# The first loads of a two-layer decoder step: smaller pieces, in another order

## The reference, cut to what matters

```
def rmsnorm(x, g):
    y = xf * rsqrt(mean(xf * xf, axis=-1) + RMS_EPS)
    return y * g

hn = rmsnorm(x, ln_mix[l])
z = hn @ w_in[l]                 # q, k, v, recurrent x, gate y, two merge gates
...                              # window attention, gated linear recurrence, merge
x = x + merged @ w_out[l]
x = x + swiglu(rmsnorm(x, ln_ffn))      # layer 0; top-2-of-8 experts in layer 1
```

## Time and profile before

| | us |
|---|---|
| median of 3 runs | 1344.1 (1343.88 to 1344.44) |
| the profiled execution, its device time | 1344.15 |
| its span from the first to the last instruction | 1342.2 |
| PE busy (matmul) | 1331.5, 99% |
| PEld busy (weight load) | 1238.8, 92% |
| DVE busy | 1053.0, 78% |
| ACT busy | 811.2, 60% |
| POOL busy | 114.2, 9% |

### The profile page before, as it was taken

One profiled execution on the slowest core, in us unless ns is written; L12 is line 12 of the kernel. 1 busy time (PEld: TensorE's weight loads), 2 busy tenths in 40 slices (PEclk: granted clock), 3 DMA queues, 4 the chain that ended last, 5 costly groups with the idle time before them and its releaser, 6 DMA issues.

```text
span 1342.2 us, 23980 instructions
## 1 busy us (share of the span) xinstructions
PE 1331.5 (99%) x8393; PEld 1238.8 (92%) x8393; DVE 1053.0 (78%) x1660; ACT 811.2 (60%) x1218; POOL 114.2 (9%) x118
## 2 busy tenths in 40 slices
PE   9999999999999999999999999999999999999997
PEld 8999999999999999999999999998888888888886
DVE  6869878876666664456698889759999999999987
ACT  6466577435333333343566784358888888888885
POOL 3200000002000000000100000021012012022010
PEclk9999999999999999999999999999999999999999
DMA  7543354445444444444533544587999999999993
GB/s 254 178 127 100 110 174 141 147 143 178 144 147 145 141 141 142 141 141 142 161 111 95 177 153 147 170 345 249 406 400 396 399 387 372 391 394 367 400 359 140
DMA packets 83258, 297.21 MB, mean 221 GB/s; under 512 B 9568, under 2 KB 11104, under 8 KB 83168
## 3 DMA queue, kind: packets, MB, share of 16 engines
q1 hardware_dynamic: 77904, 278.19, 58.3%
q0 software_dynamic: 5120, 17.67, 4.4%
q10 hardware_dynamic: 144, 0.14, 0.0%
HBM read 284.45 MB, written 11.51 MB: 221 GB/s over the span
## 4 chain that ended last, share of the span: by engine, by line
PE 97%; DVE 1%; DMA 1%; ACT 0%; issue 0%; SPq 0%; DVEq 0%; ACTq 0%
PE ps L1535 20%; PE ps L1537 20%; PE ps L1536 20%; PE ps L1876 10%; PE ps L1880 10%; PE ps L1877 10%; PE ps L1698 1%; PE ps L1635 1%; PE ps L1912 1%; PE ps L1611 1%; PE ps L1651 1%; PE ps L1867 0%; PE ps L1758 0%; DMA x<-x_in 0%; PE ps L1606 0%; PE ps L1649 0%
## 5 line engine op out<-in xcount | busy, mean ns | idle before, releaser
L1059 DVE TENSOR_TENSOR mwlo<-mraw,mwhi 128x1024 fp32r<-128x1024 f32 x290 | 343.8, 1222 | 30.4 <-ACT mwhi L577 25.7
L977 DVE TENSOR_TENSOR wlo<-raw,whi 128x1024 fp32r<-128x1024 f32 x204 | 250.3, 1228 | 125.6 <-ACT whi L577 118.6
L577 ACT ACTIVATE mwhi<-mraw 128x1024 fp32r<-128x1024 f32 x290 | 303.8, 1060 | 57.1 <-PE ps L1880 55.3
L577 ACT ACTIVATE whi<-raw 128x1024 fp32r<-128x1024 f32 (+1 forms) x208 | 216.9, 1045 | 194.8 <-DMA raw<-w_mix 128.9
L1535 PE MATMUL ps<-xuh,whi 128*128 128x336 f32 x576 | 183.7, 319 | 1.1 <-DVE xul L990 1.1
L1536 PE MATMUL ps<-xul,whi 128*128 128x336 f32 x576 | 181.7, 315 | 0.0
L1537 PE MATMUL ps<-xuh,wlo 128*128 128x336 f32 x576 | 181.5, 315 | 0.0
L1535 PE MATMUL ps<-xnh,whi 128*128 128x336 f32 (+1 forms) x544 | 174.6, 321 | 0.0
L1537 PE MATMUL ps<-xnh,wlo 128*128 128x336 f32 (+1 forms) x544 | 171.0, 314 | 0.0
L1536 PE MATMUL ps<-xnl,whi 128*128 128x336 f32 (+1 forms) x544 | 170.8, 314 | 0.0
L1876 PE MATMUL ps<-mwhi,xeh 128*128 128x512 f32 x384 | 152.9, 398 | 0.2 <-ACT xeh L577 0.2
(11 more groups left out here) (333 smaller groups left out, 2570.3 us busy)
## 6 DMA issues: line engine op xcount, KB each, us to landing
mraw<-w_moe SPq DMA_DIRECT2D x292, 512.0 KB, 8.3
raw<-w_mix SPq DMA_DIRECT2D x159, 512.0 KB, 3.5
raw<-w_ffn SPq DMA_DIRECT2D x72, 512.0 KB, 3.5
tok_d<-xt POOLq DMA_DIRECT2D x6, 224.0 KB, 3.3
ysum_d<-zero POOLq DMA_DIRECT2D x3, 448.0 KB, 11.2
ysum<-ysum_d POOLq DMA_DIRECT2D x3, 448.0 KB, 10.5
o_y<-nt SPq DMA_DIRECT2D x8, 160.0 KB, 1.9
kc<-kc_in POOLq DMA_DIRECT2D x2, 512.0 KB, 6.3
```

What stands on the lines that cost most here:

```text
L577: return nc.scalar.activation(out, in_, ACT.Copy)
L977: v.tensor_tensor(wlo[slot(c)][:, :, :], raw[slot(c)][:, :].rearrange("p (k n) -> p k n", n=P), f32(whi[slot(c)][:, :, :]), ALU.subtract). ...
L1059: v.tensor_tensor(mwlo[q % MRING][:, :, :], mraw[q % MRING][:, :].rearrange("p (k n) -> p k n", n=512), f32(mwhi[q % MSPLIT][:, :, :]), AL ...
```

## The change: what it does

The first loads are cut smaller and put in another order.

- The first half of `raw0` becomes two quarters with two tiles of `x` behind each, and the second half comes then. Tiles 2 and 3 of `x` come one by one, tiles 4 and 5 and tiles 6 and 7 in pairs as before. `raw1` comes in two halves. SP issues 11 DMAs up to the end of `raw1` instead of 8, with the same bytes.
- ACT, DVE and PE take chunk 0 in three pieces (tiles 0 and 1, 2 and 3, 4 to 7) instead of two; the first half of chunk 1 waits for its own load.
- ACT loads only 8 parameter columns first. The rest of `par` is loaded by POOL in two DMAs ahead of `kc`, `vc` and `stin`. POOL now waits for `raw1` too before its first DMA. ACT waits for the rest of `par` ahead of the root, DVE ahead of the first use.
- PE runs 8 products with zeros instead of 11.

```
-N_WARM = (11, 11, 3)
+N_WARM = (8, 11, 3)
+X_PARTS = (1, 1, 1, 1, 2, 2)
+X_PART = (0, 1, 2, 3, 4, 4, 5, 5)
...
-            sy.dma_start(raw[0][:, 0:512], w_mix[0, 0, :, 0:512]).then_inc(raw_half, 16)
-            sy.dma_start(x[:, 0:1, :], x_in[:, 0:1, :]).then_inc(x_first, 16)
+            sy.dma_start(raw[0][:, 0:256], w_mix[0, 0, :, 0:256]).then_inc(raw_quarter, 16)
+            load_x(0)
+            load_x(1)
+            sy.dma_start(raw[0][:, 256:512], w_mix[0, 0, :, 256:512]).then_inc(raw_half, 16)
+            load_x(2)
+            load_x(3)
             sy.dma_start(raw[0][:, 512:CH], w_mix[0, 0, :, 512:CH]).then_inc(raw_loaded[0], 16)
-            sy.dma_start(x[:, 1:2, :], x_in[:, 1:2, :]).then_inc(x_loaded[0], 16)
-            for q in range(1, 4):
-                sy.dma_start(x[:, 2 * q:2 * q + 2, :], x_in[:, 2 * q:2 * q + 2, :]).then_inc(x_loaded[q], 16)
-            sy.dma_start(raw[1][:, :], w_mix[0, 1]).then_inc(raw_loaded[1], 16)
+            load_x(4)
+            load_x(5)
+            sy.dma_start(raw[1][:, 0:512], w_mix[0, 1, :, 0:512]).then_inc(second_half, 16)
+            sy.dma_start(raw[1][:, 512:CH], w_mix[0, 1, :, 512:CH]).then_inc(raw_loaded[1], 16)
...
-                    pool.wait_ge(x_loaded[3], 16)
+                    pool.wait_ge(x_loaded[5], 16)
+                    pool.wait_ge(second_half, 16)
+                    pool.wait_ge(raw_loaded[1], 16)
+                    pool.dma_start(par[:, 0, 8:], par_in[:, 0, 8:]).then_inc(par_rest, 16)
+                    pool.dma_start(par[:, 1, :], par_in[:, 1, :]).then_inc(par_rest, 16)
...
-            act.dma_start(par[:, :, :], par_in).then_inc(par_loaded, 16)
+            act.dma_start(par[:, 0, 0:8], par_in[:, 0, 0:8]).then_inc(par_loaded, 16)
...
-            first_hi(0, 0)
+            first_hi(0, 0, 2, raw_quarter, hi_half)
             high(0, 0)
             high(0, 1)
-            first_hi(0, 1)
-            for k in range(2, KD):
+            first_hi(0, 2, 4, raw_half, hi_half)
+            high(0, 2)
+            high(0, 3)
+            first_hi(0, 4, 8, raw_loaded[0], hi_done)
+            for k in range(4, KD):
                 high(0, k)
-            first_hi(1, 0)
-            first_hi(1, 1)
+            first_hi(1, 0, 4, second_half, hi_half)
+            first_hi(1, 4, 8, raw_loaded[1], hi_done)
...
+                if l == 0:
+                    act.wait_ge(par_rest, 32)
                 root(2 * l)
```

More of the change, by code:

```diff
@@ L277, in build_step @@
         consts_loaded, par_loaded = sem("consts_loaded"), sem("par_loaded")
-        x_loaded = [sem(f"x_loaded{i}") for i in range(4)]
+        x_loaded = [sem(f"x_loaded{i}") for i in range(len(X_PARTS))]
         raw_loaded = [sem(f"raw_loaded{i}") for i in range(RING + 1)]
@@ L1078, in _ @@
             ve.wait_ge(par_loaded, 16)
-            first_lo(0, 0)
+            first_lo(0, 0, 2, hi_half, 1, lo_half)
             low(0, 0)
             low(0, 1)
-            first_lo(0, 1)
-            for k in range(2, KD):
+            first_lo(0, 2, 4, hi_half, 2, lo_half)
+            low(0, 2)
+            low(0, 3)
+            first_lo(0, 4, 8, hi_done, 1, lo_done)
+            for k in range(4, KD):
                 low(0, k)
-            first_lo(1, 0)
-            first_lo(1, 1)
+            first_lo(1, 0, 4, hi_half, 3, lo_half)
+            first_lo(1, 4, 8, hi_done, 2, lo_done)
             for l in range(2):
@@ L1548, in chunk @@
                 for k in range(8):
-                    if c < 2 and k in (0, 4):
-                        pe.wait_ge(lo_done if k else lo_half, c + 1)
+                    if c == 0 and k in (0, 2):
+                        pe.wait_ge(lo_half, k // 2 + 1)
+                    if c == 1 and k == 0:
+                        pe.wait_ge(lo_half, 3)
+                    if c < 2 and k == 4:
+                        pe.wait_ge(lo_done, c + 1)
                     if ready is not None:
```

25 lines of the change are left out of this document (15 added, 10 removed).

## The result

The changed kernel takes 1347.8 us (median of 10 runs, 1346.52 to 1348.83), the kernel before 1344.42 beside it (10 runs). The ratio is 1.0024 with a 95% interval of 1.0016 to 1.0032: 3.4 us slower. The forecast of 1345.0 had the sign, and a quarter of the size; the time is outside its range. The profiled execution is the slowest of the ten, 1348.83 us with a span of 1346.5.

A forecast was written before the change was run, and what follows sets the result against it. PE's chain was taken to bound 97% of the span. Chunk 1 would start 0.1 us earlier, but POOL would delay the sum, net +0.9: 1342.2 + 0.9 + 1.95 = 1345.05, or 1345.0 by the median; range 1343.7 to 1346.2.

The forecast's parts named there:

- term 1: Start of chunk 1 on PE: earlier tiles mostly offset by later ones, about 11.9 instead of 11.98, gain 0.1 us.
- Term 2: POOL's additions before the sum of squares: later start and two new DMAs, ending at 23.4; net +0.9 us.
- The bound of -0.3 us: Lower end for the gain at chunk 1's start, if the last pair of x lands 0.3 us later than forecast.
- The net does not depend on term 1: At the sum of squares: the +0.9 us holds whenever chunk 1 starts, as long as POOL is later than PE.
- Rival 2: Matrix clock stays at 1.2 GHz to the end of chunk 1 after the shorter warm-up: +4.4, 1348.5 us; chance 0.05.
- Rival 1: At the sum, POOL's last addition ends by 22.3 and PE keeps its gain: 1343.8 us; chance 0.19.
- Rival 3: Small pieces come no earlier; chunk 1 starts at 12.0 or 12.3, still 1345.0 us; chance counted within the forecast.
- Rival 4: Rest of par lands late and holds ACT's root beyond 2 us of cover: up to +1, 1346 us; chance 0.03.

The follow-up runs named there:

- e1: The changed kernel with 11 products with zeros again instead of 8; 1348.56 us, ratio 1.0031.
- e14: e1 with four more products with zeros ahead of tile 2 and four ahead of tile 4 of chunk 0; 1347.40 us, ratio 1.0025.
- e7: The kernel before with tiles 2 and 3 of x loaded one by one instead of as a pair; 1344.19 us, ratio 0.9998.
- e11: The kernel before with tiles 2 and 3 of x loaded one by one and raw1 in halves; 1343.30 us, ratio 0.9994.
- e4: The kernel before with 8 products with zeros instead of 11, nothing else; 1344.34 us, ratio 1.0005.
- e9: The kernel before with only the change's par and POOL part: eight columns first, POOL waits for raw1 and loads the rest; 1347.85 us, ratio 1.0020.
- e15: e8 with the eight-column par load issued by SP behind the first half of raw0 instead of by ACT; 1346.88 us, ratio 1.0014.
- e13: e8 with 128 par columns in the first load instead of 8; 1345.32 us, ratio 1.0007.
- e6: The changed kernel with 11 products with zeros and par loaded whole by ACT; POOL still waits for raw1; 1347.56 us, ratio 1.0020.
- e5: The changed kernel with 11 products with zeros and POOL not waiting for raw1; its two par DMAs stay; 1346.51 us, ratio 1.0014.
- e8: The kernel before with ACT loading eight par columns first and SP loading the rest behind all first loads; 1346.61 us, ratio 1.0013.
- e3: The changed kernel with 11 products with zeros and the old par load and POOL program, so the new loads alone; 1346.33 us, ratio 1.0014.
- e10: e3 with raw1 whole and tiles 2 and 3 as a pair, leaving the raw0 quarters and their order; 1345.49 us, ratio 1.0008.
- e2: The changed kernel with the old POOL program and par loaded whole by ACT, still 8 products with zeros; 1346.89 us, ratio 1.0020.
- e12: The kernel before, unchanged, run again for a second profile; 1344.26 us, ratio 0.9999.

## Why the prediction was wrong

The step that failed is the price of the cuts in term 1. It had the last pair of x 0.2 us later and `raw1` 0.5 us later, and PE at the sum 0.1 earlier. The loads from 4 to 8 us dropped by a third instead (358 to 233 GB/s), which makes PE itself late (23.22 in e1, 22.47 before) and starts POOL at 12.40 instead of 11.25. Term 2 was reckoned from a `raw1` that came too early. That the clock falls again among the first tiles was left out of the sum.

**What bounds the kernel.** Right: what reaches PE's load for the sum goes into the end whole, as the rest of 1319.7 us shows. One reading was wrong. I put the missing 0.002 of the mean clock down to the products with zeros. The stretches at the start all show 1.00 before, and the missing time lies at the end of the program, before:

```profile
1335.00:1342.00 7.00, 0.95 (x8) 0.80 (x8) 3.76 (x8) 0.00 (x0) 0.00 (x0) 0.70 0.53 187
```

0.30 of 7 us is 2.1 us, nearly all that the mean lacks. Yet the pace says that the products with zeros did run slow. Before, 22 of their records take 5.06 us, 0.23 each, and the matmul after the first real one follows 0.42 later, the next 0.24:

```profile
6.43 0.40 PE L1536 MATMUL ps<-xul,whi 128*128 128x336 f32 x1
6.67 0.31 PE L1537 MATMUL ps<-xuh,wlo 128*128 128x336 f32 x1
```

while eight such records in e14 take 0.13 each:

```profile
6.72 1.05 PE L1576 MATMUL ps<-zero 128*128 128x128 f32 x8
```

So in the first microseconds the clock column can't be trusted and the pace can. The guess that the start is slow was right, its proof by the mean was not, and I did not ask what would bring the low clock back later.

**Term 1 failed, and everything after it.** The prediction gave each added packet a cost of 30 ns beside its bytes, from two stretches with different packet sizes, took that as the whole cost of the cuts, and gave back 0.23 us for the smaller parameter load. Measured: a packet costs 9 ns beside its bytes. The 30 came out of a stretch, 4 to 5 us, in which by the packet records six packets of 1344 bytes took 404 to 554 ns each instead of 58. Single tiles of x and halves of `raw1` cost nothing that can be seen (e7, e11), while the small parameter load or the quarters of `raw0` with their order take the loads between 4 and 8 us from 358 to 376 GB/s down to 264 to 302, and both together to 233 to 261. The term I credited with +0.23 us is one of the two that hurt. `raw1` landed at 11.7 where I had 11.0, and chunk 1 started at 12.70 in a run without low clock (e1) and at 14.36 in the profile of the changed kernel, where I had 11.9 and bounds of 11.4 to 12.3. The bound of -0.3 us came from the same model of packets as the value, so it could not hold what the model left out.

**Term 2 was right in its mechanism, with a start too early.** POOL's five DMAs took 3.30 us in the forecast and 12.40 to 15.65 = 3.25 in the trace; the two new ones 1.27 instead of 1.12, `kc` 0.92 instead of 1.06. POOL started at 12.40 instead of 11.25: 0.7 by the later landing of `raw1`, and 0.4 because the DMA begins 0.69 us after that landing (11.71) and not 0.25. From the first addition to the last end I had 8.85 us; it took 9.56, since three of the seven additions were long (1.64, 1.70, 1.71), not two; in e1, without the low clock, it took 8.91. Together 25.3 instead of 23.4. The wait of PE was 1.34 in e1, where 1.0 was forecast, but on top of a PE that was 0.75 late by itself. "The net does not depend on term 1" was the sentence that hid this: POOL's start hangs on the same landing of `raw1` as term 1.

**Rival 2, at 0.05, was real in part.** The low clock is real in the profile after, and its sign for recognition (matmuls 0.3 us apart after 11 us) is met. The shorter warm-up is not what decides it: the clock does fall in e4 with 8 products, from 7.7 to 11.1 and at a price of 0.4 to 1.0, but it falls for longer in e9, with 11 products. Nor does it reach through chunk 1 at +4.4, as I priced it; it ends with chunk 0 and costs PE 1.6, and in this profile POOL is later still (25.30 against 24.80). The 1.4 in the router it did not name at all. That its 1348.5 lies near the measured 1347.8 is luck. What goes with the fall are gaps of PE up to and among the first tiles, in e9 because the operands are late. I had named them ("more gaps between the first tiles") and then set them aside with "the operands of chunk 0 come so densely", which was the old kernel's profile. The gaps ahead of matmuls in us, from the end of the first products with zeros on, and the start of the first matmul that is slow again:

| profile | gaps | low from |
|---|---|---|
| after | 0.76, 1.25 | 7.73 |
| e4 | 1.29, 0.64 | 7.70 |
| e9 | 0.17, 2.18 | 8.45 |
| e15 | 0.97, 0.32, 0.52 | 9.67 |
| e13 | 1.21, 0.39 | 9.95 |
| e6 | 0.70, 0.35, 2.05 | 10.99 |
| e5 | 1.51, 0.29, 0.92 | 11.02 |
| e8 | 0.21, 1.72, 0.40 | stays high |
| e3 | 1.05, 1.47 | stays high |
| e1 | 1.32, 1.34 | stays high |
| e10 | 0.82, 1.52, 0.44 | stays high |
| e2 | 0.61, 0.54, 0.17, 1.46 | stays high |
| before | 0.27, 0.84 | stays high |

The length of the longest gap does not decide: the clock falls in e15, with none over 0.97, and stays in e8, with one of 1.72. The Trainium skill ("TensorE: Matmul & The Clock Gate", Part 1, HAM oscillation) describes waits for loads between groups of matmuls that let the clock fall again; its example has much longer waits than these, and there every group starts slow. The traces agree that the clock falls behind such waits, but with shorter ones, and not in every profile. That the gaps are the cause is argued from this and not shown: the five profiles with no gap over 0.84 (before, e7, e11, e12, e14) all stay high, and e14 has more runs at high clock than e1, but too few to settle it. I had cited the part and only used its sentence on the warm-up.

**The two delays stand side by side, not in a row.** In the changed kernel PE is ready at 24.80 and POOL at 25.30. The profile without low clock still has POOL (e1: 24.56), and the one with POOL in time has the clock (e5: 24.49 with POOL done at 22.58). Only without both does PE come near 22.9 (e2, e3). So e1 alone would have told me, falsely, that the clock doesn't matter.

**Rivals 1, 3 and 4.** Rival 1 needed an early `raw1`; nothing of it is seen. Rival 3 is right that the small pieces start chunk 1 no earlier (12.70 in e1, against its 12.3 at most), but its time of 1345.0 is not. Rival 4 did not come: the rest of `par`, issued at 12.4 and 13.1, was in time: no wait for it stands in the chain.

**The size.** At high clock the whole costs +3.0 us, without a disturbance (e1): 1.4 by the loads (e3), 1.1 to 1.6 by POOL's wait for `raw1` (e6 against e3, e1 against e5), up to 0.5 by the `par` DMAs behind that wait (e1 against e6). Of this 0.3 us lies outside the span, in the four kernels where POOL waits for `raw1` and loads `par` (2.3 us instead of 2.0: the change, e1, e9, e14). With the `par` loads alone it is 2.1 (e5), with the wait alone 2.05 (e6); why both together cost it stays open. The sum closes: the kernel before at high clock takes 1343.6 to 1343.8, and less 2.0 outside and a rest of 1319.6 this puts its load for the sum at 22.0 to 22.2, an estimate; e12 has 21.92. PE ready 1.0 to 1.2 later in e1, 1.34 of waiting for POOL and 0.3 outside are 2.6 to 2.8 of the +3.0. The runs at lower mean clock take 1.0 to 3.0 us more than the others of their kernel, and there are more of them: 8 of 10 for the change, 47 of 119 for the kernel before. In profiles the router at 905 us has 1.2 to 2 us of that. It shows the low clock in single executions of either order; why those would come more often with this start stays open.

## What to carry to other kernels

A load cut smaller is not just the same bytes plus a price for each packet: look at GB/s over the first stretches after the change, and try each cut by itself, since two of the four pieces here were harmless, and the two others (one of them with its order) slowed what was queued behind them. Where several engines meet at one point, write down each one's time of arrival before and after; a change that makes two of them late by the same amount can't be repaired one at a time. And gaps ahead of the first matmuls may cost more than themselves, if the clock falls with them; read the pace of the matmuls, and not only the clock.

## What the runs showed of the hardware

- With an early load of 32 bytes for each partition in place of 1056 the large ones behind it are slower: 285 GB/s between 4 and 8 us instead of 358 and 368, with the engines busy for 0.96 of the time (e8). With 512 bytes it is 302 (e13), from SP's queue 285 (e15), and quarters of `raw0` in the new order with the whole `par` give 271 (e10). From 2 to 4 us the difference is small (271 instead of 297 and 283).
- A DMA packet takes 9 ns and 0.037 ns a byte of its engine (9 ns at 32 bytes, 159 at 4096, medians before and after). The rate drops by single packets that are held up, in e6 one for 2.1 us.
- The granted clock fell to 0.50 near gaps of 1.25 us (the changed kernel, at 7.7) and 2.18 us (e9), and behind three gaps of 0.97, 0.32 and 0.52 us (e15), and stayed at 1.00 through gaps of 1.72 us (e8) and 1.47 us (e3). In the changed kernel it was back at 14.4, when PE had worked since 10.9.
- The clock column shows 1.00 before the first rise too: in the kernel before, matmuls at 6.01 and 6.43 stand 0.42 apart and those from 9.09 to 9.40 0.15, in stretches that both read 1.00.
- POOL's addition of 128x336 takes 0.92 us alone and 1.64, 1.70 and 1.71 beside a subtraction of DVE with two operands in the changed kernel, 1.59 and 1.98 before.
